# A decoder layer with seven-product blocks: which engine forms the four weight sums, and in which order the products run

## The reference, cut to what matters

```python
D_MODEL, SEQ, FFN_DIM = 2048, 256, 5632

def swiglu(x, w_gate, w_up, w_down):
    return (jax.nn.silu(x @ w_gate) * (x @ w_up)) @ w_down

h = swiglu(rms_norm(x, ffn1_pre_g), ffn1_w_gate, ffn1_w_up, ffn1_w_down)
x = x + 0.5 * rms_norm(h, ffn1_post_g)
...
h = swiglu(rms_norm(x, ffn2_pre_g), ffn2_w_gate, ffn2_w_up, ffn2_w_down)
x = x + 0.5 * rms_norm(h, ffn2_post_g)
```

## Time and profile before

| | us |
|---|---|
| median of 3 runs | 1798.53 |
| lowest, highest | 1797.92, 1799.12 |
| the profiled execution, its own time | 1797.71 |
| its span in the trace | 1796.0 |
| PE busy | 1746.8 (97%) |
| DVE busy | 1376.9 (77%) |
| ACT busy | 1005.2 (56%) |
| POOL busy | 75.8 (4%) |
| units SECOND to LAST of GU1 | 127.53 to 472.53 |
| units SECOND to LAST of GU2 | 1189.28 to 1535.00 |

### The profile page before, as it was taken

One profiled execution on the slowest core, in us unless ns is written; L12 is line 12 of the kernel. 1 busy time (PEld: TensorE's weight loads), 2 busy tenths in 40 slices (PEclk: granted clock), 3 DMA queues, 4 the chain that ended last, 5 costly groups with the idle time before them and its releaser, 6 DMA issues. The chain is left out here.

```text
span 1796.0 us, 20689 instructions
## 1 busy us (share of the span) xinstructions
PE 1746.8 (97%) x7938; PEld 1436.7 (80%) x7938; DVE 1376.9 (77%) x1174; ACT 1005.2 (56%) x947; POOL 75.8 (4%) x95
## 2 busy tenths in 40 slices
PE   9999999999999999999999999999999999999998
PEld 7887777777788888788888878887777777788886
DVE  7877778888688988665578468877788877688887
ACT  6645556666555655543347445655565556555553
POOL 1000000000000000010000000000000000000000
PEclk9999999999999999999999999999999999999999
DMA  8857777888766554365541556867778887666453
GB/s 331 317 184 246 246 247 249 252 254 253 228 230 229 194 211 166 138 230 184 181 166 53 186 184 255 293 182 247 249 248 253 255 255 232 234 234 227 167 194 116
DMA packets 70186, 395.11 MB, mean 220 GB/s; under 512 B 6368, under 2 KB 6624, under 8 KB 41696
## 3 DMA queue, kind: packets, MB, share of 16 engines
q1 hardware_dynamic: 59888, 344.77, 50.5%
q0 software_dynamic: 10080, 49.29, 14.3%
q10 hardware_dynamic: 144, 0.04, 0.0%
HBM read 389.88 MB, written 4.19 MB: 219 GB/s over the span
## 5 line engine op out<-in xcount | busy, mean ns | idle before, releaser
L1530 DVE TENSOR_TENSOR op_lo<-quads,op_hi 128x2560 fp32r<-128x2560 f32 x126 | 354.0, 2820 | 143.1 <-ACT op_hi L1008 143.1
L1008 ACT ACTIVATE op_hi<-quads 128x2560 fp32r<-128x2560 f32 x126 | 295.6, 2346 | 206.2 <-DMA quads<-in_paired 147.9
L2259 PE MATMUL banks<-w_hi,act_hi 128*128 128x512 f32 (+1 forms) x1008 | 396.2, 393 | 2.1 <-DVE act_lo L1495 1.5
L2261 PE MATMUL banks<-w_hi,act_lo 128*128 128x512 f32 (+1 forms) x1008 | 390.9, 388 | 0.0
L2260 PE MATMUL banks<-w_lo,act_hi 128*128 128x512 f32 (+1 forms) x1008 | 390.6, 387 | 0.0
L2482 PE MATMUL banks<-w_hi,hid_split 128*128 128x512 f32 x992 | 277.5, 392 | 4.7 <-DVE hid_split L1783 4.7
L1484 DVE TENSOR_TENSOR w_lo<-raw,w_hi 128x2048 fp32r<-128x2048 f32 (+3 forms) x75 | 162.1, 2162 | 130.8 <-ACT w_hi L924 130.8
L924 ACT ACTIVATE w_hi<-raw 128x2048 fp32r<-128x2048 f32 (+3 forms) x75 | 136.0, 1813 | 205.1 <-PE banks L2261 200.0
L2482 PEld LDWEIGHTS banks<-w_hi,hid_split 128*128 128x128 f32 x992 | 187.4, 189 | 45.3 <-DVE hid_split L1783 6.4
L1177 ACT ACTIVATE w_hi<-raw 128x2048 fp32r<-128x2048 f32 x63 | 120.8, 1917 | 181.8 <-PE banks L2482 180.6
L2259 PEld LDWEIGHTS banks<-w_hi,act_hi 128*128 128x128 f32 x1008 | 189.7, 188 | 40.7 <-issue 2.3
(11 more groups left out here) (221 smaller groups left out, 2471.0 us busy)
## 6 DMA issues: line engine op xcount, KB each, us to landing
raw<-in_weights SPq DMA_DIRECT2D x131, 1024.0 KB, 4.8
quads<-in_paired SPq DMA_DIRECT2D x72, 1280.0 KB, 8.0
quads<-in_paired POOLq DMA_DIRECT2D x36, 1280.0 KB, 10.3
raw<-in_weights SPq DMA_DIRECT2D x40, 768.0 KB, 5.8
w_tail<-in_weights SPq DMA_DIRECT2D x36, 768.0 KB, 7.3
raw<-in_paired SPq DMA_DIRECT2D x32, 768.0 KB, 5.7
ahead<-in_weights SPq DMA_DIRECT2D x8, 1024.0 KB, 10.2
rows<-in_x SPq DMA_DIRECT2D x4, 1024.0 KB, 11.1
```

The costliest lines, as they stand in the source:

```text
L1008: nc.scalar.activation(op_hi[op_slot(v, op)][:, :], op_raw(op), ACT.Copy)\
L1530: nc.vector.tensor_tensor(op_lo[:, slot, :], op_raw(op), op_hi[slot][:, :], ALU.subtract)\
L2259: nc.tensor.matmul(out_ap, hi, rhs_hi, start=start, stop=False, skip_group_check=chain)
L2261: return nc.tensor.matmul(out_ap, lo, rhs_hi, start=False, stop=stop, skip_group_check=chain)
```

## The change

Each unit still has the same seven products, four plain pieces and four sums, but three of the sums are made in another way:

- `sum3` (R22 += R12) becomes an adding transfer of GpSimd's, from R12's DRAM rows, as soon as P3's low part has read R22.
- `sum1` (R12 += R11) stays an adding transfer. It is issued right behind that one, when R12 has landed.
- `sum2` (R11 += R22) stays on VectorE and waits for the first transfer.
- `sum4` becomes a GpSimd `tensor_tensor` over 128x2560, R21 += R11, after P2's low part and `sum2`. P4 reads it in R21's place.

PE's order becomes P3, P1, L_A, P2, turn, L_B, P7, P6, L_C, P5, P4, turn, L_D. The order of ScalarE, VectorE and SyncE follows, and the loads of R11, R12 and R21 change places. In the down projection VectorE makes the low parts of piece 0 ahead of the first operand's. The cut diff:

```diff
-MADE = {L_A: -1, O_P6: 0, L_B: 1, L_C: 2, O_P2: 3, O_P5: 4, L_D: 5, O_P4: 6}
-USED = {L_A: 0, O_P6: 1, L_B: 2, O_P2: 3, L_C: 4, O_P5: 5, O_P4: 6, L_D: 7}
+MADE = {L_A: -1, L_B: 0, O_P2: 1, O_P6: 2, L_C: 3, O_P5: 4, O_P4: 5, L_D: 6}
+USED = {L_A: 0, O_P2: 1, L_B: 2, O_P6: 3, L_C: 4, O_P5: 5, O_P4: 6, L_D: 7}
...
-OP_RAW = {O_P1: R11, O_P3: R22, O_P7: R22, O_P6: R11, O_P5: R12, O_P2: R21, O_P4: R11}
+OP_RAW = {O_P1: R11, O_P3: R22, O_P7: R22, O_P6: R11, O_P5: R12, O_P2: R21, O_P4: R21}
...
                 behind = unit_behind(v)
+                if v is not FIRST:
+                    sp.wait_ge(lo_ready, made(stage, v, L_B))
+                    load_plain(stage, v, L_D)
                 sp.wait_ge(op_lo_ready, per_unit(stage, v.u, 3, OP_COUNT[O_P7]))
                 load_quad(stage, behind, R22)
                 if v is not FIRST:
-                    sp.wait_ge(lo_ready, made(stage, v, L_B))
-                    load_plain(stage, v, L_D)
                     sp.wait_ge(lo_ready, made(stage, v, L_C))
                     load_plain(stage, behind, L_A)
-                sp.wait_ge(lo_ready, made(stage, v, O_P2))
-                load_quad(stage, behind, R21)
+                else:
+                    sp.wait_ge(lo_ready, made(stage, v, O_P6))
+                sp.wait_ge(sum_ready, per_unit(stage, v.u, 2, 2))
+                load_quad(stage, behind, R11)
                 sp.wait_ge(lo_ready, made(stage, v, O_P5))
                 load_quad(stage, behind, R12)
+                sp.wait_ge(lo_ready, made(stage, v, O_P4))
+                load_quad(stage, behind, R21)
+                sp.wait_ge(lo_ready, made(stage, v, L_D))
+                load_plain(stage, behind, L_B)
...
             def add_quads(stage, v):
-                pool.wait_ge(sum_ready, per_unit(stage, v.u, 2, 1))
+                pool.wait_ge(op_lo_ready, per_unit(stage, v.u, 3, OP_COUNT[O_P3]))
+                nc.gpsimd.dma_start(quad_raw(R22), paired[bass.ds(quad_row(stage, v, R12), 1), :, :]
+                                    .rearrange("o p n -> (o p) n"), accum_op=ALU.add,
+                                    max_dma_last_dim=2 * OPERAND).then_inc(sum3_landed, 16)
+                pool.wait_ge(pair_landed[R12], v.u * 16 + 16 * ffn(stage) * QUAD_LOADS)
                 nc.gpsimd.dma_start(quad_raw(R12), paired[bass.ds(quad_row(stage, v, R11), 1), :, :]
                                     .rearrange("o p n -> (o p) n"), accum_op=ALU.add,
                                     max_dma_last_dim=2 * OPERAND).then_inc(sum1_landed, 16)
-                pool.wait_ge(lo_ready, made(stage, v, O_P6))
-                nc.gpsimd.dma_start(quad_raw(R11), paired[bass.ds(quad_row(stage, v, R21), 1), :, :]
-                                    .rearrange("o p n -> (o p) n"), accum_op=ALU.add,
-                                    max_dma_last_dim=2 * OPERAND).then_inc(sum4_landed, 16)
+                pool.wait_ge(lo_ready, made(stage, v, O_P2))
+                pool.wait_ge(sum_ready, per_unit(stage, v.u, 2, 1))
+                nc.gpsimd.tensor_tensor(quad_raw(R21), quad_raw(R21), quad_raw(R11), ALU.add).then_inc(sum_ready, 1)
...
+                elif op == O_P2:
+                    act.wait_ge(op_used, per_unit(stage, v.u, 3, OP_COUNT[O_P3]))
                 elif op == O_P7:
-                    act.wait_ge(sum_ready, per_unit(stage, v.u, 2, 1))
-                    act.wait_ge(op_used, per_unit(stage, v.u, 3, OP_COUNT[O_P3]))
+                    act.wait_ge(sum3_landed, per_unit(stage, v.u, 16, 16))
+                    act.wait_ge(op_used, per_unit(stage, v.u, 3, OP_COUNT[O_P1]))
...
                 elif op == O_P4:
-                    act.wait_ge(sum4_landed, per_unit(stage, v.u, 16, 16))
-                    act.wait_ge(piece_used, used(stage, v, O_P2))
+                    act.wait_ge(sum_ready, per_unit(stage, v.u, 2, 2))
+                    act.wait_ge(piece_used, used(stage, v, O_P6))
...
-            def sum3(stage, v):
-                dve.wait_ge(pair_landed[R12], v.u * 16 + 16 * ffn(stage) * QUAD_LOADS)
-                nc.vector.tensor_tensor(quad_raw(R22), quad_raw(R22), quad_raw(R12), ALU.add).then_inc(sum_ready, 1)
             def sum2(stage, v):
-                dve.wait_ge(sum_ready, per_unit(stage, v.u, 2, 1))
+                dve.wait_ge(sum3_landed, per_unit(stage, v.u, 16, 16))
...
                 sum_sides(stage, 0)
+                take_both_down(stage, 0)
                 down_operand_low(stage, 0)
-                take_both_down(stage, 0)
...
                 plain_product(stage, v, L_A, before)
+                product(stage, v, O_P2)
+                turn_hidden(stage, near_block(before))
+                plain_product(stage, v, L_B, before)
                 product(stage, v, O_P7)
                 product(stage, v, O_P6)
-                turn_hidden(stage, near_block(before))
-                plain_product(stage, v, L_B, before)
-                product(stage, v, O_P2)
                 plain_product(stage, v, L_C, before)
```

More of the change, by code:

```diff
@@ L187 @@
 SIDE_A11, SIDE_SUMS, SIDE_REST = range(3)
-QUAD_AT = {R22: 0, R11: 1, R12: 2, R21: 3}
-DOWN_QUAD_AT = {R12: 0, R21: 1, R11: 2, R22: 3}
-OP_RAW = {O_P1: R11, O_P3: R22, O_P7: R22, O_P6: R11, O_P5: R12, O_P2: R21, O_P4: R11}
+QUAD_AT = {R22: 0, R11: 1, R21: 2, R12: 3}
+DOWN_QUAD_AT = {R22: 0, R11: 1, R21: 2, R12: 3}
+OP_RAW = {O_P1: R11, O_P3: R22, O_P7: R22, O_P6: R11, O_P5: R12, O_P2: R21, O_P4: R21}
 DOWN_RAW = {O_P1: R11, O_P3: R22, O_P7: R22, O_P6: R11, O_P5: R12, O_P2: R21, O_P4: R21}
@@ L701, in load_units @@
                     sp.wait_ge(rows_spilled, 16 * TILES)
-                for n, q in enumerate((R22, R11, R12, R21)):
+                for n, q in enumerate((R22, R11, R21, R12)):
                     sp.wait_ge(lo_ready, stage + 9 + n)
@@ L716, in load_units @@
                 load_plain(stage, TAIL, L_A)
-                sp.wait_ge(lo_ready, made(stage, LAST, O_P5))
+                sp.wait_ge(sum_ready, per_unit(stage, LAST.u, 2, 2))
                 load_down_quad(down_stage, 0, R11)
                 load_down_quad(down_stage, 0, R22)
+                sp.wait_ge(lo_ready, made(stage, LAST, O_P4))
+                load_down_quad(down_stage, 0, R21)
+                load_down_quad(down_stage, 0, R12)
                 sp.wait_ge(lo_ready, made(stage, LAST, L_D))
                 load_plain(stage, TAIL, L_B)
-                sp.wait_ge(lo_ready, made(stage, LAST, O_P4))
-                load_down_quad(down_stage, 0, R12)
-                load_down_quad(down_stage, 0, R21)
                 sp.wait_ge(lo_ready, made(stage, TAIL, L_A))
@@ L1079, in unit @@
                 behind, before = unit_behind(v), FIRST if v is SECOND else unit_before(v)
+                plain_high(stage, v, L_B)
                 keep_p3(stage, v)
+                operand_high(stage, v, O_P2)
+                begin_near(stage, v)
                 operand_high(stage, v, O_P7)
-                begin_near(stage, v)
+                gate_near(stage, before, v)
                 operand_high(stage, v, O_P6)
-                plain_high(stage, v, L_B)
-                gate_near(stage, before, v)
                 plain_high(stage, v, L_C)
+                keep_hidden(stage, near_block(before))
                 keep_p7(stage, v)
-                operand_high(stage, v, O_P2)
                 operand_high(stage, v, O_P5)
-                keep_hidden(stage, near_block(before))
+                operand_high(stage, v, O_P4)
                 plain_high(stage, v, L_D)
-                operand_high(stage, v, O_P4)
                 gate_far(stage, before, v)
@@ L1585, in first_unit @@
                 operand_low(stage, SECOND, O_P1)
-                sum3(stage, SECOND)
             def unit(stage, v, last=False):
                 behind, before = unit_behind(v), FIRST if v is SECOND else unit_before(v)
+                plain_low(stage, v, L_B)
+                operand_low(stage, v, O_P2)
                 sum2(stage, v)
+                multiply_hidden(stage, near_block(before), near_bank(before))
                 operand_low(stage, v, O_P7)
                 operand_low(stage, v, O_P6)
-                plain_low(stage, v, L_B)
-                multiply_hidden(stage, near_block(before), near_bank(before))
                 plain_low(stage, v, L_C)
-                operand_low(stage, v, O_P2)
+                operand_low(stage, v, O_P5)
                 begin_near(stage, v)
-                operand_low(stage, v, O_P5)
+                operand_low(stage, v, O_P4)
                 plain_low(stage, v, L_D)
-                operand_low(stage, v, O_P4)
                 multiply_hidden(stage, far_block(before), FAR_BANK)
                 plain_low(stage, behind, L_A)
+                if not last:
+                    operand_low(stage, behind, O_P3)
                 begin_far(stage, v)
                 if not last:
-                    operand_low(stage, behind, O_P3)
                     operand_low(stage, behind, O_P1)
```

(2 more changed lines are left out.)

49 lines of the change are left out of this document (19 added, 30 removed).

## The result

The changed kernel took **1813.64 us** (median; 1810.17 to 1814.40), beside 1798.82 us of the kernel before (1797.92 to 1802.31). The ratio is 1.0075, with a 95% interval of 1.0056 to 1.0094: it is slower by 0.75%, where the prediction had 1790.4 us and a range that ended at 1801. Both the sign and the range were wrong.

A forecast was written before the change was run, and what follows sets the result against it. It took PE's 41.5 us of waits, set by a ring of transfers through R11, as the bound. Units won 7.1, FIRST lost 2.0, down projections won 3.0: 8.1 off the 1798.53 median gives 1790.4 us, range 1753 to 1801.

The forecast's parts named there:

- What bounds the kernel: PE's waits in two stretches of eight units cost 41.5 us, paced by a ring of adding transfers and copies through R11.
- `sum3` as a transfer: In each unit the transfer lands 8.5 us after P3's product starts, so `sum2` waits nothing, with 0.9 us to spare.
- P7 waits 2.15, and 0.1 for the slower restart: Ahead of P7 in each unit PE waits 2.0 us for its low part, plus 0.1 for restart: 2.15 us.
- the predicted 34.4: Sum over 16 units of the 2.15 us wait ahead of P7: 34.4 us instead of 41.5, so 7.1 won.
- GpSimd's addition: The new 2560-column addition behind `sum2` takes 5.8 us, hand-overs included.
- rival 2: GpSimd's addition takes longer, 7.8 us, so P7's low part makes a unit wait 4.15 us: 1826 us; chance 0.13.
- The block: GpSimd's SBUF reads and VectorE's two-operand instructions exclude each other both ways, so P7's low part waits until 18.05 us; chance 0.45.
- Rival 1: GpSimd's addition holds up nothing that matters, P7's low part ends by 18.7 us, the waits vanish: 1755.5 us; chance 0.33.
- FIRST: In each stage's FIRST unit, P7 or P6 is delayed 0 to 2.15 us; 1.0 taken per stage, 2.0 us lost.
- The down projections: Ahead of piece 0 in each down stage, taking its low parts earlier wins 1.5 us, 3.0 in all.
- The range: 1753 to 1801 us, down to the no-waits time less 2 us, up to the no-change case's end.

## Why the prediction was wrong, point by point

**What bounds the kernel: right.** 41.5 us of waits were there to be won, and 1750.6 us (1798.5 - 41.5 - 6.5 = 1750.5) shows that they can be, nearly to the last. That GpSimd issued one adding transfer at a time was right as well; enlarging the space showed the reason, which the prediction did not have.

***`sum3` as a transfer*: the step that failed first.** "It lands at 8.5, hidden by 0.9" took 9.4 to 10.3 us from transfers at another place of the unit. The issue came when predicted, 1.8 us ahead of P3's product; the landing did not. At its new place the loads of L_B and L_C are under way when it issues (R21's has just landed) and L_D's follows, and it took 9.7 to 13.6 us, median 12.2 and 11.6. In GU1 the median landing was thus 10.4 us behind P3's product instead of 8.5. Holding L_C and L_D brought it to 9.6, and with it the whole unit to the predicted shape. The trace of before held the warning: the other adding transfer (L885), with loads beside it, took 11.5 to 13.8 us in the units from SECOND on. The view of it, with both FIRST:

```profile
DMA to landing us min/median/max: 9.4/12.5/13.8
```

The unit of the earlier trace rows shows one, issued at 364.73 and awaited by P4's high copy until 376.48. The prediction took the landing time from L881 alone. The prediction's last sentence named a landing of over 11 us as what would break it, but gave it no case, no price and no chance. Its own sum held the price: every microsecond of landing beyond the 0.9 of slack is one of PE's wait, ahead of P7 or of the turn, in each of 16 units, since P7's low part has no lead left. The waits came to 45.7 us instead of 32.8. The Trainium skill (DMA: Bandwidth & Descriptors, § Issuing engines are not separate DMA queues) says that transfers of SP and of GpSimd run on the same 16 DMA engines and interleave. The run with L_C and L_D held agrees: with two of SP's loads out of the way the median landing in GU1 fell from 12.2 to 9.6 us.

***P7 waits 2.15, and 0.1 for the slower restart*: the second step that failed.** The wait alone is 1.82 us where the transfer is in time, and so right. The restart was taken as a constant from the small waits of before. Behind longer ones the granted clock fell to half for 3.4 or 6.8 us in 8 of 16 units: 17.4 us instead of 1.6. The trace of before showed it where the down projections begin: behind 2.12 us of idle time, the length that the earlier trace rows has, piece 0's matmuls took 7.19 us at a mean clock of 0.76, and 5.61 at full clock in after. The prediction read the idle time there and not the rows behind it. Of the 28.7 us that the units cost above the predicted 34.4, longer waits are 12.9 and this term 15.8; and the longer waits bring the lower clock, so the two steps are not independent. Filling the wait with matmuls took all such stretches away.

**GpSimd's addition: right.** 5.71 us (5.8 predicted), it starts 0.1 us after `sum2`, and the time is not set by it alone: rival 2 wanted an addition of over 6.3 us for the slower side. The loss against before came at 5.71, with the other two terms on top of the block that the prediction had priced.

**The block: right, in both directions.** P7's low part starts beside the addition and ends 2.7 us after it, 7.8 us long. In FIRST it is the addition that takes 8.16 us, because P7's low part went first. The Trainium skill (SBUF — State Buffer, § Who interferes with whom) has an instruction with two SBUF inputs contend with one of GpSimd that reads SBUF; these lengths agree. Rival 1 (no block) was thus wrong as a mechanism, but its time, 1755.5, is near that of the kernels in which the addition is cut or moved to VectorE (1750.1 and 1750.6).

**FIRST:** 1.2 us lost in two stages, 2.0 predicted. **The down projections:** 6.5 us won, 3.0 predicted, again because of the clock behind the idle time.

**The range** went with the terms whose ends it took. Its upper end assumed that only the addition's length could be wrong; a landing 1 to 3 us later than in the earlier trace rows had no place in it.

## What to carry to other kernels

A transfer that is moved gets a new landing time: take it from transfers of its kind that have as much under way beside them as it will have at the new place, not from its old rows, and price a few microseconds more wherever its successor has no slack. When you cost a wait of PE, read also the rows behind a wait of that length, for the granted clock; a wait of 2 to 3 us cost up to twice its length here. Before giving an addition to GpSimd, look for a spot where VectorE has slack: here 2.82 us of VectorE were free, and 5.7 us of GpSimd, which block VectorE's two-operand work, cost 63 us on the other side (34 with the loads held, so that the transfer is in time and the clock stays up).

## What the runs showed of the hardware

- From SECOND on, an adding transfer of 1.25 MB landed after 9.3 to 10.6 us with L_C's and L_D's loads held, and after 9.7 to 13.6 us in after. The bulk of its bytes was hardly slower in the late cases; a few packets at the end were. Two stretches of after during the transfer that landed at 367.18 (columns as above, with the weight loads in place of the matmuls): the DMA share falls from full to a third while the transfer is awaited.

```profile
354.20:364.20 10.00, 8.27 (x45) 1.00 1.01 250
364.20:367.18 2.98, 2.48 (x14) 1.00 0.34 130
```

  This fits some of the 16 engines finishing later than the others; that is a reading of the share, as these views do not tell the engines apart. Which they are, and why only in some units, is open.
- With room for 1024 in the space for descriptors, GpSimd's second adding transfer issues 0.3 us after the first has landed; with 1792, 0.7 us after the first has issued. (In FIRST it waits for R12 in either case.) Side by side the second takes 17.4 to 19.5 us instead of 9.5 to 9.9, counted from its issue, and lands 18.1 to 20.3 us behind the first's issue instead of 19.8 to 23.3: the two share the engines, and what is won is little.
- The same kernel had the half clock in 8 of 16 units in both of its profiled executions, in partly other ones. Behind the common wait of P7, 1.8 us from start to start (1.7 as counted), it stood in no unit of any trace of the new order. With both loads held it stood in one unit, SECOND of GU1, behind 1.95 us from start to start; in three other units with 1.94 or 1.95 it did not. With the addition on VectorE it stood in none.
